# Sparse attention in whole steps: another order of scores, copies, masks and exponentials on three engines

## The chip, the cores and the metric

The kernel runs on one core of a Trainium2 chip. The metric is the device time of one execution in microseconds, the median of several runs.

## The reference

A two-layer decoder trunk over 1024 positions of width 1024, in float32. Layer 0 has latent attention with a convolution beside it, layer 1 native sparse attention; each is followed by a mixture of 32 experts. The change lies in the sparse attention of layer 1. It has 16 heads of width 64 in two groups that share keys and values. The two branches of it that matter here are, cut to their core:

```python
# selected blocks: 8 of 16 blocks of 64 keys for every query
s = einsum('bghqd,bgqnld->bghqnl', qc, kg) * DK ** -0.5 - slopes * dist
p = softmax(where(valid, s, NEG_INF))
o_slc = einsum('bghqnl,bgqnld->bghqd', p, vg)
# sliding window: the last 256 keys
s = einsum('bghqd,bgkd->bghqk', qc, kb) * DK ** -0.5 - slopes * dist
o_win = einsum('bghqk,bgkd->bghqd', softmax(where(valid, s, NEG_INF)), vb)
o = g[0] * o_cmp + g[1] * o_slc + g[2] * o_win
```

## The kernel before, in words

`attend` is called twice: by `mla_attention` for layer 0 (one branch a step, named mlaatt in the trace) and by `nsa_attention` for layer 1 (two branches, nsaatt). A step is one pair of heads (h = 0, 1) and one tile of 128 queries. The sparse attention has 8 pairs, and in each the tiles in the order 0, 7, 1, 6, 2, 5, 3, 4, so 64 steps in 8 rounds. Branch 0, the selected blocks, is computed over all t + 1 causal blocks of 128 keys with a mask that leaves out what wasn't chosen; branch 1, the window, over at most three blocks. A step is *wide* when branch 0 has more than 512 columns (tiles 4 to 7), else *narrow*; wide and narrow steps alternate, and step s + 4 is of the same kind as step s.

The work of a step, by engine:

- TensorE, `score(s, r)`: two or more matmuls into PSUM for branch r and both heads (line 1031). Each head has two banks; a wide branch 0 fills both, a narrow one the first, and the window always uses the second. So a score waits on `masked`, a count of masks that VectorE has done.
- VectorE, `mask(s, i)`, i = 2r + h: adds the mask, takes the maximum, and writes the result from PSUM to `probs` (line 1125). `biased(s, r)` makes the bias of the exponential from the maximum (line 1134).
- ScalarE, `exps(s, r, h)`: the exponential with its sum (line 1083), after `bias_ready`.
- VectorE, `inverse(s, r)`: reciprocal of the sum (line 1139), after `exp_done`. GpSimd scales `probs` with it and the gate (line 1112).
- TensorE, `turn(n)`: transposes a group of up to two blocks and both heads into one of three PSUM banks (line 1041). It needs the scaled rows and the copy of group n - 3.
- ScalarE or VectorE, `copy_group`: copies a transposed group to SBUF (line 1087 on ScalarE, 1005 on VectorE). `by_act[n] = n % 4 != 2`, so VectorE has every fourth group. A round has 34 groups: steps of tiles 0, 7, 1, 6, 2, 5, 3, 4 have 2, 6, 2, 6, 4, 5, 4, 5 of them. Which group of a tile is VectorE's therefore repeats every second round.
- TensorE, `value(n)`: the group's values (line 1054), after its copy; the first of a step waits for the `add` of the step before, since one bank holds the values.
- VectorE, `add(s)`: adds the values to the output (line 1145).

Every engine works its queue strictly in the order of the program. The steps overlap: while TensorE has the values of step s, it makes the scores of step s + AHEAD (4 in the sparse attention, 3 in layer 0), and ScalarE has the exponentials of s + 3. An opening loop fills the first four steps. The loop over s then issues for each step:

| engine | order before, narrow step | order before, wide step |
|---|---|---|
| TensorE | score(s+4, 0), score(s+4, 1), values(s), turns(s+1) | score(s+4, 0), values(s), score(s+4, 1), turns(s+1) |
| ScalarE | four exps(s+3), then its copies(s+1) | the same |
| VectorE | masks 0, 1, 2, biased 0, mask 3, add, both inverses, biased 1, copies | masks 0, 1, add, biased 0, masks 2, 3, both inverses, biased 1, copies |

After a stage's block all engines meet; then `project_out` follows, and the experts' weights of layer 1 are issued behind it on SyncE.

Of the kernel before, what the change touches and what calls it, by code (L numbers as in the profile page):

```python
# [952 lines left out]
def attend(nc, name, steps, ident, loads=None, prepare=None, room=None):  # L953

    S = len(steps)
    BR = len(steps[0]["branches"])
    SUB = 2 * BR
    LAST = BR - 1
    AHEAD = 3 if BR == 1 else 4
# [7 lines left out]
    first = np.cumsum([0] + [len(g) for g in groups]).tolist()  # L967
# [5 lines left out]
    def wide(s):  # L973
        return BR > 1 and steps[s]["branches"][0]["blocks"] * P > BANK

    with Phase(nc, name) as ph:
        probs = ph.sb("probs", [P, BUFS, 2, WIDE])
        outside = room.shape[1] // BANK if room is not None else 0
# [28 lines left out]
        with nc.Block() as block:  # L1007
# [6 lines left out]
            def _(pe):  # L1014
# [47 lines left out]
                for n in range(first[1]):  # L1062
                    turn(n)
                for s in range(S):
                    if s + AHEAD < S:
                        score(s + AHEAD, 0)
                        if BR > 1 and not wide(s + AHEAD):
                            score(s + AHEAD, 1)
                    for n in range(first[s], first[s + 1]):
                        value(n)  # L1070
                    if s + AHEAD < S and wide(s + AHEAD):
                        score(s + AHEAD, 1)
                    if s + 1 < S:
                        for n in range(first[s + 1], first[s + 2]):
                            turn(n)

            @block.scalar
            def _(act):
                def exps(s, r, h):
                    if h == 0:  # L1080
                        act.wait_ge(bias_ready, BR * s + r + 1)
                    b, i = s % BUFS, 2 * r + h
                    act.activation(part(s, r, h), part(s, r, h), ACT.Exp, bias=bias[:, b, i:i + 1], scale=steps[s]["scale"][h],  # L1083
                                   accum_out=total[:, b, i:i + 1]).then_inc(exp_done, 1)

                def copy(to, source):
                    return act.activation(to, source, ACT.Copy)  # L1087

                for s in range(AHEAD - 1):
                    for i in range(SUB):  # L1090
                        exps(s, i // 2, i % 2)
                for n in range(first[1]):
                    if by_act[n]:
                        copy_group(act, copy, n, copied_act)
                for s in range(S):
                    if s + AHEAD - 1 < S:
                        for i in range(SUB):
                            exps(s + AHEAD - 1, i // 2, i % 2)
                    if s + 1 < S:
                        for n in range(first[s + 1], first[s + 2]):  # L1100
                            if by_act[n]:
                                copy_group(act, copy, n, copied_act)

            @block.gpsimd
            def _(pool):
# [10 lines left out]
            def _(dve):  # L1116
# [29 lines left out]
                    else:  # L1146
                        dve.tensor_copy(to, o_ps[:, 0:P]).then_inc(added, 1)

                def copies(s):
                    for n in range(first[s], first[s + 1]):  # L1150
                        if not by_act[n]:
                            copy_group(dve, dve.tensor_copy, n, copied_dve)

                for s in range(AHEAD):
                    for i in range(SUB):
# [3 lines left out]
                    if s:  # L1159
                        for r in range(BR):  # L1160
                            inverse(s - 1, r)
                copies(0)
                for s in range(S):
                    ahead = s + AHEAD < S
                    if ahead:
                        mask(s + AHEAD, 0)
                        mask(s + AHEAD, 1)
                        if BR > 1 and not wide(s + AHEAD):
                            mask(s + AHEAD, 2)
                            biased(s + AHEAD, 0)  # L1170
                            mask(s + AHEAD, 3)
                    add(s)
                    if ahead and wide(s + AHEAD):
                        biased(s + AHEAD, 0)
                        mask(s + AHEAD, 2)
                        mask(s + AHEAD, 3)
                    if s + AHEAD - 1 < S:
                        for r in range(BR):
                            inverse(s + AHEAD - 1, r)
                    if ahead:  # L1180
                        biased(s + AHEAD, LAST)
                    if s + 1 < S:
                        copies(s + 1)


def mla_attention(nc, q_cols, k_cols, v_rows, causal, o_cols, ident, rows_to_clear, loads):
# [1880 lines left out]
```

## Time and profile before

| what | value |
|---|---|
| median of 3 runs | 2205.34 us (2203.54 to 2207.75) |
| the profiled execution, its time | 2202.24 us |
| its span in the trace | 2200.4 us |
| TensorE busy | 1979.2 us |
| sparse attention, both branches | 1320.9 to 1712.2 us |

The times are those of whole executions; the profile is of one of them. A wait in a row of a timeline stands in square brackets: how long the engine was idle before the instruction, and what, by the trace, ended it. Where an engine waits for several semaphores the row names the one that came last by the trace's reckoning, and that can be another than the one that held it. Matmul counts in the trace are passes: a score or value matmul in float32 is two of them, a transpose one.

### The profile page before, as it was taken

Reading aid. Unit: us, or ns where it says so; the run is one execution under the profiler, and the core shown is the slowest. Engines: PE = TensorE matmul, PEld = TensorE weight load, DVE = VectorE, ACT = ScalarE, POOL = GpSimd, SP = SyncE. Lnnn points to the kernel's source line nnn. Section 1 sums busy time; section 2 is a strip of 40 time slices with the busy share of each in tenths; the row PEclk is TensorE's granted clock in tenths of the full one; section 3 lists DMA queues with packets and bytes.
Section 4 is the critical chain, followed back from the end, with each engine's and each line's share of the span. In section 5 each row is a group of like instructions: output and inputs, shape, how many; then the busy total and the mean of one; then the engine's idle time right before and its main releaser. Section 6 shows DMA issues by size and latency. Waiting matters only on the chain. (4 is left out here: it accounts for less than half of the span.)

```text
span 2200.4 us, 30381 instructions
## 1 busy us (share of the span) xinstructions
PE 1979.2 (90%) x11293; PEld 1263.0 (57%) x11293; DVE 951.5 (43%) x2308; ACT 701.0 (32%) x1765; POOL 457.3 (21%) x619
## 2 busy tenths in 40 slices
PE   6999859999999998959999768999999999999887
PEld 3444435655587665645655535666666557766664
DVE  3896974433261211114223486666665125321111
ACT  4013554531111111112122475767666111111110
POOL 0001002331022222100000264445445001222111
PEclk8999969999989999979999988999999999999998
DMA  5000001132588999862000200001000515999992
GB/s 220 0 0 0 0 16 52 36 94 109 211 315 305 375 376 364 307 215 43 1 0 1 80 1 11 11 11 49 11 11 20 195 68 197 340 360 379 377 356 75
DMA packets 80889, 307.78 MB, mean 140 GB/s; under 512 B 18352, under 2 KB 23495, under 8 KB 63846
## 3 DMA queue, kind: packets, MB, share of 16 engines
q1 hardware_dynamic: 66342, 272.23, 32.2%
q0 software_dynamic: 14400, 33.59, 6.2%
q8 instruction: 93, 1.52, 0.3%
q14 instruction: 54, 0.44, 0.1%
HBM read 276.75 MB, written 47.89 MB: 148 GB/s over the span
## 5 line engine op out<-in xcount | busy, mean ns | idle before, releaser
L1112 POOL TENSOR_SCALAR nsaatt_probs<-nsaatt_probs,nsaatt_inv,trunk_gates_or_logits 128x384 f32<-128x384 f32 (+7 forms) x256 | 185.6, 739 | 202.1 <-DVE nsaatt_inv L1139 202.1
L1125 DVE CUSTOM_DVE_ANT_0 nsaatt_probs<-nsaatt_scores,trunk_arena 128x384 f32<-128x384 f32 (+7 forms) x256 | 151.3, 629 | 87.8 <-PE nsaatt_scores L1031 87.5
L1761 DVE TENSOR_TENSOR experts_sig<-experts_gu_ps,experts_sig 128x256 f32<-128x256 f32 x50 | 21.2, 425 | 356.2 <-ACT experts_sig L1718 356.2
L1083 ACT ACTIVATE nsaatt_probs<-nsaatt_probs,nsaatt_bias 128x384 f32<-128x384 f32 (+7 forms) x256 | 169.0, 667 | 11.8 <-DVE nsaatt_bias L1134 11.7
L1594 PEld LDWEIGHTS experts_gu_ps<-experts_x_cols,ahead 128*128 128x128 f32 x1408 | 159.1, 192 | 8.9 <-issue 8.9
L1594 PE MATMUL experts_gu_ps<-experts_x_cols,ahead 128*128 128x128 f32 x1408 | 161.6, 276 | 2.8 <-ACT experts_x_cols L1713 2.8
L1031 PE MATMUL nsaatt_scores<-layer_k_cols,trunk_x_rows 64*128 64x384 f32 (+3 forms) x640 | 131.1, 521 | 15.7 <-DVE nsaatt_top L1125 12.8
L1041 PE MATMUL nsaatt_turn<-trunk_ident,nsaatt_probs 128*128 128x128 f32 x912 | 123.8, 279 | 23.5 <-POOL nsaatt_probs L1112 6.0
L1718 ACT ACTIVATE experts_sig<-experts_gu_ps 128x256 f32<-128x256 f32 x50 | 19.2, 383 | 369.3 <-PE experts_gu_ps L1594 242.5
L1041 PEld LDWEIGHTS nsaatt_turn<-trunk_ident,nsaatt_probs 128*128 128x128 f32 x912 | 97.3, 140 | 57.4 <-issue 37.7
L2239 PE MATMUL nsain_q_ps<-trunk_arena,l1b_h_cols 128*128 128x512 f32 x256 | 111.7, 594 | 0.0
L268 DVE SCALAR_TENSOR_TENSOR l0a_conv<-layer_v_rows,l0a_taps,l0a_conv 128x1024 f32<-128x1024 f32 x87 | 104.8, 1282 | 0.0
L1477 POOL DMA_INDIRECT moe_x<-h_rows,moe_index x46 | 47.5, 1033 | 244.2 <-PE experts_x_ps L1575 229.7
L563 DVE TENSOR_TENSOR trunk_x_rows<-out_acc,trunk_x_rows 128x512 f32<-128x512 f32 x32 | 22.1, 692 | 171.8 <-PE out_acc L491 171.8
L1087 ACT ACTIVATE trunk_arena<-nsaatt_turn 128x512 f32<-128x512 f32 (+1 forms) x136 | 65.8, 514 | 79.7 <-PE nsaatt_turn L1041 79.1
L1031 PEld LDWEIGHTS nsaatt_scores<-layer_k_cols,trunk_x_rows 64*128 64x128 f32 x640 | 55.1, 195 | 60.4 <-issue 37.1
L1722 ACT ACTIVATE trunk_x_rows<-experts_y_ps,moe_gates 128x512 f32<-128x512 f32 x50 | 34.4, 687 | 149.7 <-PE experts_y_ps L1636 75.0
L1054 PE MATMUL nsaatt_values<-trunk_arena,layer_v_rows 128*64 128x128 f32 x1228 | 81.8, 276 | 0.0
L2239 PEld LDWEIGHTS nsain_q_ps<-trunk_arena,l1b_h_cols 128*128 128x128 f32 x256 | 48.2, 190 | 58.0 <-issue 57.9
L1636 PE MATMUL experts_y_ps<-ahead,experts_hid 128*128 128x512 f32 x176 | 79.3, 593 | 2.0 <-DVE trunk_x_rows L1789 2.0
L1031 PE MATMUL mlaatt_scores<-layer_k_cols,trunk_x_rows 96*128 96x512 f32 (+3 forms) x192 | 74.9, 530 | 5.1 <-DVE mlaatt_top L1125 4.1
L1789 DVE TENSOR_SCALAR trunk_x_rows<-experts_y_ps,moe_gates 128x512 f32<-128x512 f32 x50 | 37.4, 748 | 94.6 <-PE experts_y_ps L1636 32.6
(444 smaller groups left out, 3804.2 us busy)
## 6 DMA issues: line engine op xcount, KB each, us to landing
ahead<-in_moe_w_gate_dram SPq DMA_DIRECT2D x34, 1024.0 KB, 14.3
ahead<-in_moe_w_up_dram SPq DMA_DIRECT2D x34, 1024.0 KB, 20.8
ahead<-in_moe_w_down_dram SPq DMA_DIRECT2D x34, 1024.0 KB, 22.1
trunk_arena<-in_moe_w_gate_dram SPq DMA_DIRECT2D x10, 1024.0 KB, 14.0
trunk_arena<-in_moe_w_up_dram SPq DMA_DIRECT2D x10, 1024.0 KB, 18.5
trunk_arena<-in_moe_w_down_dram SPq DMA_DIRECT2D x10, 1024.0 KB, 25.9
moe_w<-in_moe_w_gate_dram SPq DMA_DIRECT2D x10, 1024.0 KB, 12.5
moe_w<-in_moe_w_up_dram SPq DMA_DIRECT2D x10, 1024.0 KB, 23.4
```

The costliest lines, as they stand in the source:

```text
L268: ins = dve.scalar_tensor_tensor(out=to, in0=shifted, scalar=w, in1=to, op0=ALU.mult, op1=ALU.add)
L1031: last = pe.matmul(scores_of(s, r, h)[:, lo:hi], st["q"][h], br["k"][h](lo, hi), start=True, stop=True)
L1041: last = pe.transpose(t_ps[n % TURNS][:, (h * (hi - lo) + b - lo) * P:(h * (hi - lo) + b - lo + 1) * P], part(s, r, h)[:, b * P:(b + 1) * ...
L1054: last = pe.matmul(o_ps[h * V_DIM:(h + 1) * V_DIM, 0:P], br["v"][h](b), turned_probs[n % PT_BUFS][:, at:at + P], start=(r == 0 and b == 0) ...
L1083: act.activation(part(s, r, h), part(s, r, h), ACT.Exp, bias=bias[:, b, i:i + 1], scale=steps[s]["scale"][h], accum_out=total[:, b, i:i + ...
L1087: return act.activation(to, source, ACT.Copy)
L1112: pool.tensor_scalar(part(s, r, h), part(s, r, h), inv[:, s % BUFS, i:i + 1], 1.0 if gate is None else gate[h], ALU.mult, ALU.mult).then_i ...
L1125: dve.tensor_tensor_reduce(part(s, r, h), scores_of(s, r, h), br["mask"], 1.0, -3e38, ALU.add, ALU.max, top[:, s % BUFS, i:i + 1]).then_in ...
L1477: pool.indirect_dma_start(out=x_rows[:, s, :], out_offset=None, in_=h_dram, in_offset=bass.IndirectOffsetOnAxis(ap=rows.bitcast(U32), axis=0),
L1594: last = pe.matmul(to, wm[:, c, half * P:(half + 1) * P], x_cols[:, b, c, :], start=(c == 0), stop=(c == CHUNKS - 1))
L1636: last = pe.matmul(y_ps[half][:, :], hid[:, b, c * P:(c + 1) * P], wm[:, c, half * BANK:(half + 1) * BANK], start=(c == 0), stop=(c == 1))
L2239: last = pe.matmul(to, h_cols[:, c, t * P:(t + 1) * P], w_in[:, c, lo:hi], start=(c == 0), stop=(c == CHUNKS - 1))
```

## The change

Orders alone change, in the loop over s; instructions, buffers and the opening loop are the same. In a step of the sparse attention:

| engine | order after, narrow step | order after, wide step |
|---|---|---|
| TensorE | score(s+4, 0), values(s), score(s+4, 1), turns(s+1) | score(s+4, 0), values(s), turns(s+1), score(s+4, 1) |
| ScalarE | exps 0, 1, two copies, exps 2, one copy, exps 3, the rest | exps 0, 1, 2, copies (five at most), exps 3, the rest |
| VectorE | masks 0 to 3, first copy, biased 0, inverse 0, add, other copies, inverse 1, biased 1 | masks 0, 1, biased 0, add, inverse 0, first copy, mask 2, other copies, mask 3, inverse 1, biased 1 |

With one branch (layer 0) the code has a case of its own, `BR == 1`, with two masks or exponentials in a step.

```diff
+    def copied_by(s, act):
+        return [n for n in range(first[s], first[s + 1]) if by_act[n] == act] if s < S else []
...
                 for s in range(S):
-                    if s + AHEAD < S:
+                    ahead = s + AHEAD < S
+                    if ahead:
                         score(s + AHEAD, 0)
-                        if BR > 1 and not wide(s + AHEAD):
-                            score(s + AHEAD, 1)
                     for n in range(first[s], first[s + 1]):
                         value(n)
-                    if s + AHEAD < S and wide(s + AHEAD):
+                    if ahead and BR > 1 and not wide(s + AHEAD):
                         score(s + AHEAD, 1)
                     if s + 1 < S:
                         for n in range(first[s + 1], first[s + 2]):
                             turn(n)
+                    if ahead and wide(s + AHEAD):
+                        score(s + AHEAD, 1)
...
                 for s in range(S):
-                    if s + AHEAD - 1 < S:
-                        for i in range(SUB):
-                            exps(s + AHEAD - 1, i // 2, i % 2)
-                    if s + 1 < S:
-                        for n in range(first[s + 1], first[s + 2]):
-                            if by_act[n]:
-                                copy_group(act, copy, n, copied_act)
+                    mine = copied_by(s + 1, True)
+                    if BR == 1:
+                        exp_ahead(s, 0)
+                        exp_ahead(s, 1)
+                        copies(mine)
+                    elif wide(s):
+                        exp_ahead(s, 0)
+                        exp_ahead(s, 1)
+                        exp_ahead(s, 2)
+                        copies(mine[:5])
+                        exp_ahead(s, 3)
+                        copies(mine[5:])
+                    else:
+                        exp_ahead(s, 0)
+                        exp_ahead(s, 1)
+                        copies(mine[:2])
+                        exp_ahead(s, 2)
+                        copies(mine[2:3])
+                        exp_ahead(s, 3)
+                        copies(mine[3:])
...
                 for s in range(S):
-                    ahead = s + AHEAD < S
-                    if ahead:
-                        mask(s + AHEAD, 0)
-                        mask(s + AHEAD, 1)
-                        if BR > 1 and not wide(s + AHEAD):
-                            mask(s + AHEAD, 2)
-                            biased(s + AHEAD, 0)
-                            mask(s + AHEAD, 3)
-                    add(s)
-                    if ahead and wide(s + AHEAD):
-                        biased(s + AHEAD, 0)
-                        mask(s + AHEAD, 2)
-                        mask(s + AHEAD, 3)
-                    if s + AHEAD - 1 < S:
-                        for r in range(BR):
-                            inverse(s + AHEAD - 1, r)
-                    if ahead:
-                        biased(s + AHEAD, LAST)
-                    if s + 1 < S:
-                        copies(s + 1)
+                    mine = copied_by(s + 1, False)
+                    mask_ahead(s, 0)
+                    mask_ahead(s, 1)
+                    if BR == 1:
+                        add(s)
+                        inverse_ahead(s, 0)
+                        biased_ahead(s, 0)
+                        copies(mine)
+                    elif wide(s):
+                        biased_ahead(s, 0)
+                        add(s)
+                        inverse_ahead(s, 0)
+                        copies(mine[:1])
+                        mask_ahead(s, 2)
+                        copies(mine[1:])
+                        mask_ahead(s, 3)
+                        inverse_ahead(s, 1)
+                        biased_ahead(s, 1)
+                    else:
+                        mask_ahead(s, 2)
+                        mask_ahead(s, 3)
+                        copies(mine[:1])
+                        biased_ahead(s, 0)
+                        inverse_ahead(s, 0)
+                        add(s)
+                        copies(mine[1:])
+                        inverse_ahead(s, 1)
+                        biased_ahead(s, 1)
```

`exp_ahead`, `mask_ahead`, `biased_ahead` and `inverse_ahead` call the old functions for step s + 3 or s + 4, where there is one; `copies` now takes a list of groups.

## Rows read from the trace of the kernel before

**Rows 1.** The page's first part: busy time of each engine.
```profile
PE 1979.2 (90%) x11293; PEld 1263.0 (57%) x11293; DVE 951.5 (43%) x2308; ACT 701.0 (32%) x1765; POOL 457.3 (21%) x619
```
**Rows 2.** Windows of the sparse attention: whole stage, then its steady part.
```profile
core 0: us, PE busy (x) PEld busy (x) DVE busy (x) ACT busy (x) POOL busy (x), PEclk, DMA share, GB/s
1320.90:1712.20 391.30, 354.55 (x3376) 250.75 (x3376) 241.40 (x912) 262.12 (x716) 185.61 (x256) 0.97 0.06 18
1345.00:1700.00 355.00, 326.85 (x3186) 234.11 (x3184) 225.09 (x848) 246.01 (x673) 175.19 (x241) 1.00 0.06 19
```
**Rows 3.** Waits of TensorE, 1344 to 1712 us: total, times, longest.
```profile
PE nsaatt_scores L1031 <- DVE nsaatt_top L1125: 6.0, 14, 0.5
PE nsaatt_turn L1041 <- POOL nsaatt_probs L1112: 6.0, 8, 1.3
PE nsaatt_turn L1041 <- DVE trunk_arena L1005: 5.7, 6, 1.6
PE nsaatt_turn L1041 <- ACT trunk_arena L1087: 4.5, 8, 0.7
PE nsaatt_turn L1041 <- DVE nsaatt_probs_cols L1005: 3.5, 4, 1.8
PE nsaatt_turn L1041 <- ACT nsaatt_probs_cols L1087: 2.4, 4, 0.7
```
**Rows 4.** Waits of TensorE, 1320 to 1344 us (the opening loop).
```profile
PE nsaatt_scores L1031 <- DVE nsaatt_top L1125: 6.8, 5, 2.6
```
**Rows 5.** Timeline of TensorE: start, length, line, operation, count, wait before it.
```profile
1497.89 2.96 PE L1041 MATMUL nsaatt_turn<-trunk_ident,nsaatt_probs 128*128 128x128 f32 x20
1500.77 1.35 PE L1031 MATMUL nsaatt_scores<-layer_k_cols,trunk_x_rows 64*128 64x512 f32 x8
...
1504.39 0.92 PE L1031 MATMUL nsaatt_scores<-layer_k_cols,trunk_x_rows 64*128 64x384 f32 x4
1505.23 1.31 PE L1041 MATMUL nsaatt_turn<-trunk_ident,nsaatt_probs 128*128 128x128 f32 x10
1507.35 0.41 PE L1041 MATMUL nsaatt_turn<-trunk_ident,nsaatt_probs 128*128 128x128 f32 x2 [0.80 <-POOL nsaatt_probs L1112]
...
1512.00 0.84 PE L1041 MATMUL nsaatt_turn<-trunk_ident,nsaatt_probs 128*128 128x128 f32 x6 [0.68 <-DVE trunk_arena L1005]
...
1529.42 0.92 PE L1031 MATMUL nsaatt_scores<-layer_k_cols,trunk_x_rows 64*128 64x384 f32 x4 [0.41 <-DVE nsaatt_top L1125]
...
1530.85 1.56 PE L1031 MATMUL nsaatt_scores<-layer_k_cols,trunk_x_rows 64*128 64x384 f32 x8
1532.34 0.66 PE L1054 MATMUL nsaatt_values<-nsaatt_probs_cols,layer_v_rows 128*64 128x128 f32 x8
1532.93 1.53 PE L1041 MATMUL nsaatt_turn<-trunk_ident,nsaatt_probs 128*128 128x128 f32 x12
1536.11 1.28 PE L1041 MATMUL nsaatt_turn<-trunk_ident,nsaatt_probs 128*128 128x128 f32 x10 [1.64 <-DVE trunk_arena L1005]
```
**Rows 6.** Timeline of VectorE and ScalarE around two of those waits.
```profile
1506.51 0.69 DVE L1005 COPY nsaatt_probs_cols<-nsaatt_turn 128x512 f32<-128x512 f32 x1
...
1531.28 1.04 ACT L1083 ACTIVATE nsaatt_probs<-nsaatt_probs,nsaatt_bias 128x896 f32<-128x896 f32 x1
...
1533.33 0.61 ACT L1083 ACTIVATE nsaatt_probs<-nsaatt_probs,nsaatt_bias 128x384 f32<-128x384 f32 x1
...
1533.33 0.55 DVE L1125 CUSTOM_DVE_ANT_0 nsaatt_probs<-nsaatt_scores,trunk_arena 128x384 f32<-128x384 f32 x1
...
1534.53 1.07 ACT L1087 ACTIVATE trunk_arena<-nsaatt_turn 128x512 f32<-128x512 f32 x2
1534.67 0.17 DVE L1139 RECIPROCAL nsaatt_inv<-nsaatt_total 128x2 f32<-128x2 f32 x1 [0.50 <-ACT nsaatt_probs L1083]
...
1535.28 0.68 DVE L1005 COPY trunk_arena<-nsaatt_turn 128x512 f32<-128x512 f32 x1
```
**Rows 7.** Timeline of SyncE: the first expert weight load of layer 1.
```profile
1716.45 0.43 SPq L1301 DMA_DIRECT2D ahead<-in_moe_w_gate_dram  x1
```

More of the change, by code:

```diff
@@ L1094, in _, with exp_ahead, copies @@
                         copy_group(act, copy, n, copied_act)
-                for s in range(S):
-                    if s + AHEAD - 1 < S:
-                        for i in range(SUB):
-                            exps(s + AHEAD - 1, i // 2, i % 2)
-                    if s + 1 < S:
-                        for n in range(first[s + 1], first[s + 2]):
-                            if by_act[n]:
-                                copy_group(act, copy, n, copied_act)
+                def exp_ahead(s, i):
+                    if s + AHEAD - 1 < S:
+                        exps(s + AHEAD - 1, i // 2, i % 2)
+                def copies(groups):
+                    for n in groups:
+                        copy_group(act, copy, n, copied_act)
+                for s in range(S):
+                    mine = copied_by(s + 1, True)
[18 more added lines that the diff above has]
+                        copies(mine[3:])
             @block.gpsimd
@@ L1147, in add, with copies @@
                         dve.tensor_copy(to, o_ps[:, 0:P]).then_inc(added, 1)
[L1149 to L1152, printed above, removed]
+                def copies(groups):
+                    for n in groups:
+                        copy_group(dve, dve.tensor_copy, n, copied_dve)
                 for s in range(AHEAD):
@@ L1161, in _ @@
                             inverse(s - 1, r)
-                copies(0)
-                for s in range(S):
-                    ahead = s + AHEAD < S
-                    if ahead:
-                        mask(s + AHEAD, 0)
-                        mask(s + AHEAD, 1)
-                        if BR > 1 and not wide(s + AHEAD):
-                            mask(s + AHEAD, 2)
-                            biased(s + AHEAD, 0)
-                            mask(s + AHEAD, 3)
-                    add(s)
-                    if ahead and wide(s + AHEAD):
-                        biased(s + AHEAD, 0)
-                        mask(s + AHEAD, 2)
-                        mask(s + AHEAD, 3)
-                    if s + AHEAD - 1 < S:
-                        for r in range(BR):
-                            inverse(s + AHEAD - 1, r)
-                    if ahead:
-                        biased(s + AHEAD, LAST)
-                    if s + 1 < S:
-                        copies(s + 1)
+                copies(copied_by(0, False))
@@ new lines, in mask_ahead, with biased_ahead, inverse_ahead @@
+                def mask_ahead(s, i):
+                    if s + AHEAD < S:
+                        mask(s + AHEAD, i)
+                def biased_ahead(s, r):
+                    if s + AHEAD < S:
+                        biased(s + AHEAD, r)
+                def inverse_ahead(s, r):
+                    if s + AHEAD - 1 < S:
+                        inverse(s + AHEAD - 1, r)
+                for s in range(S):
+                    mine = copied_by(s + 1, False)
[26 more added lines that the diff above has]
+                        biased_ahead(s, 1)
```

## The prediction

> **What bounds the kernel.** I read the page first: TensorE is busy 90% of the span, no other engine over 43% [rows 1]. The diff only acts inside the sparse attention, so the next view is the windows: that stage takes 391.3 us, TensorE is busy 354.55 of them and stands at its full clock (1.00) from 1345 to 1700 us, where it is busy 326.85 of 355 us; VectorE, ScalarE and GpSimd are at 62%, 67% and 47% [rows 2]. So TensorE sets the stage's end, and a change of order that leaves its instructions alone can only return its gaps. The waits say how much there is: from 1344 us on, six kinds of wait add up to 28.1 us (6.0 + 6.0 + 5.7 + 4.5 + 3.5 + 2.4): 14 waits of the scores for masks, 30 of the transposes [rows 3]. The 6.8 us of score waits before that [rows 4] belong to the opening loop, which the diff leaves as it is.
>
> Twelve of the 44 waits make up two rounds over the eight tiles: 0.80, 0.68, 0.46, 0.50, 0.41, 1.64 us in one, 0.52, 0.29, 0.46, 0.68, 0.41, 0.75 in the next (four of them, the largest too, are in [rows 5]), 7.6 us together. Rounds differ because a round has 34 groups and every fourth group is VectorE's. I call a round "even" when VectorE has the first and fifth group of tiles 7 and 6, "odd" when it has their third. The wait of 1.64 us is of an even round.
>
> The waits put down to GpSimd are not GpSimd's. The one at 1507.35 us [rows 5] ends 0.15 us after a VectorE copy (1506.51 + 0.69 = 1507.20) [rows 6], and the fourth group must have the first one's copy, since three PSUM banks hold transposes. All 30 waits of transposes are of this kind: a copy stands behind exponentials, masks or reciprocals on its own engine.
>
> **Part 1, wide steps (32 of 64): window scores after the transposes.** Before, a score waits 0.46 or 0.41 us for the masks of its own step, as at 1529.42 us [rows 5]; those 14 waits (6.0 us) go, since the masks are long done when the next step's transposes end. What is late next: these masks start later, and the next narrow step's window scores need them. They come after that step's selected scores and values, at the least 0.65 + 0.59 = 1.24 us later (tile 0, whose partner is tile 2), elsewhere 1.7 us or more. Two masks of 384 columns take 2 x 0.48 us plus 0.2 us of signalling, 1.2 us. It just fits; I allow 0.05 us a step, 1.6 us in all.
>
> With the window scores out of the way, the narrow step's transposes follow the values at once. For tile 2 in an odd round (the 0.80 us wait): values end at 1504.39 us, group 1 some 0.55 us later; VectorE does its add and one reciprocal meanwhile, copies 0.69 us and is done at 1505.8; the fourth group would be reached at 1505.65. About 0.25 us is left of 0.80.
>
> **Part 2, narrow steps (32): window scores after the values.** No instruction is added, but one more run of score matmuls is: a run of 384 columns alone takes 0.84 us (1504.39 to 1505.23), two joined take 1.49 us (1530.85 to 1532.34), so standing alone costs 1.68 - 1.49 = 0.19 us [rows 5]. In a wide step the window scores now run straight into the next step's selected scores, which joins two runs and returns the same 0.19 us. Sum 0; if joining returns nothing, 32 x 0.19 = 6 us lost; if the split costs nothing and joining pays, 6 us won. I take 0, since both prices come from the same two rows. The Trainium skill (TensorEngine Tiling (Array Packing), Key Properties) says that a change of tiling mode drains TensorE; scores use 64 rows, values 64 columns, transposes the whole array. By that rule a narrow step gets one switch more and a wide step one less, the same 0; read as a warning against the split alone it would make the sum 6 us worse, and the trace's 0.19 us agrees with a drain.
>
> **Part 3, ScalarE's copies between its exponentials.** In the worst wait, a narrow step of tile 0 ahead of tile 7: ScalarE does four exponentials, 1531.28 to 1534.53 us, and then two copies [rows 6]. Now it copies after two, at about 1533.35 us or as soon as a group is turned. That is before the fourth group can need it (1534.35, the end of twelve transposes from 1532.93) [rows 5]. The cost is that the last two exponentials end some 1 to 2 us later; cover: their reciprocal feeds GpSimd, whose results are wanted by transposes a whole step later (a pair of steps takes about 11.8 us), and GpSimd is idle for half of the stage. Without that cover it would cost up to 1 us a pair.
>
> **Part 4, VectorE's order.** In the same step the copy of the first group starts at 1535.28 us, behind four masks, the add, both reciprocals (the second waits 0.50 us for ScalarE) and the biases [rows 6]; TensorE goes on at 1536.11 us, 1.64 us late [rows 5]. Afterwards: selected scores alone to 1531.7, values 0.59 to 1532.3, window scores 0.84 to 1533.1, then the transposes. Masks 3 and 4 follow the window scores: 1533.25 + 2 x 0.48 = 1534.2; copy 0.69 to 1534.9; TensorE goes on at 1535.0 and wanted to at 1534.5. So 0.5 us is left of 1.64. In an odd round the first copy is ScalarE's and nothing is left of 0.75. For tile 6, in an even round the same 0.5 us is left. Its twenty transposes hide a wait that no view lists: they take 1497.89 to 1500.77, 2.88 us, where the pitch of 0.115 us and 0.14 us of run-out (twelve transposes are shown with 1.53 us) make 2.44 [rows 5]; 0.44 x 8 rounds = 3.5 us more to be had. For tiles 5 and 4 the first copy comes 1.2 us or more earlier (two exponentials of 0.61 us on ScalarE [rows 6]), against waits of 0.29 to 0.68: nothing and about 0.1 us are left.
> The moved add costs nothing: values of the next step want it only after its scores, 1.3 us or more behind the transposes.
>
> **The sum.** To be had: 28.1 + 3.5 = 31.6 us. Left in two rounds: 0.25 + 0.5 + 0.1 (odd tile 2, even tile 7, tile 4) and 0.5 + 0.15 (tiles 6 and 4 again), 1.5 us, times 4 = 6.0 us. Narrow window scores 1.6 us. Gain 31.6 - 6.0 - 1.6 = 24.0 us. The first attention, with one branch, gets its old order back line for line: 0. After the stage everything is issued behind it in program order, the expert weights too (1716.45 us) [rows 7], so the gain isn't eaten by loads that start at a fixed time; the two loads inside the stage have a DMA share of 0.06 around them [rows 2]. The profiled execution took 2202.24 us (span 2200.4) against a median of 2205.34, 3.1 us or 0.14% apart, so I subtract from the median: 2205.3 - 24 = 2181.3 us, stage about 367 us.
>
> **The rivals.**
> 1. *Half of it* (0.20). VectorE's copies stay late in both kinds of round, since the masks of the window scores now come just when the first group is turned. Then only the score waits (6.0 us) and those put down to ScalarE (4.5 + 2.4) go: 12.9 us, 2192 us. For: the even rounds' remainder above. Against: in odd rounds ScalarE has the first group.
> 2. *The waits only move* (0.06). Values of a wide step need all copies, the last now stand behind the fourth exponential; if TensorE waits there what it waited before, 2205 us. Against: the last copy ends at about 1.6 us into the next step, whose scores and first values take longer.
> 3. *Slower: the narrow window scores wait for VectorE* (0.10). The wide step's masks 3 and 4 now stand behind its transposes and a copy, and the bank is needed 1.24 us later at the earliest. Each 0.1 us by which they are late on all 32 narrow steps costs 3.2 us; from 0.75 us late it eats the 24 us. One 0.69 us copy and a 0.5 us wait for an exponential in front of them make 1.2 us: 2181 + 1.15 x 32 = 2218 us. Against: VectorE is idle 38% of the stage.
> 4. *The likeliest* (0.64): 2181 us, by itself 2173 to 2189 (all waits gone: 31.6 us, 2174; runs of scores dearer by 6 us: 2187).
>
> Range 2173 to 2197: all of the likeliest and rival 1 with some 5 us above it. Measurement can't tell less than 0.2% (4.4 us) from no change. Faster: 0.64 + 0.20 = 0.84; same 0.06; slower 0.10.
>
> **What would show it.** Score waits of 0.4 us gone from the stage; no wait of a transpose over about 0.6 us; the sum of TensorE's waits from 1344 us on down from 28 to 6 to 8 us; runs of eight score matmuls in which 384 columns lead into the next step's; TensorE's busy time within 2 us of 354.55; stage 367 us. I am wrong if scores wait for masks in narrow steps, if values wait for copies, or if TensorE's busy time grows by the 6 us of the extra runs.

## The result, and the profile after

The changed kernel takes 2180.64 us (median of 4 runs, 2177.89 to 2183.09) against 2204.44 us for the kernel before on the same chips: ratio 0.9886, interval 0.9868 to 0.9904, a gain of 23.8 us. The prediction was 2181.3 us.

The page first. TensorE does the same instructions as before [rows 1] and is now busy 91% of a shorter span; the span is 2176.2 us.

```profile
PE 1975.6 (91%) x11293; PEld 1263.9 (58%) x11293; DVE 958.0 (44%) x2308; ACT 700.3 (32%) x1765; POOL 460.0 (21%) x619
```

The windows of the sparse attention, whole and steady, with the columns of [rows 2]. The whole stage takes 366.3 us where it took 391.3; in the steady part TensorE is busy 327.82 of 335 us, 7.2 us short of all, where it was 28 us short of 355. TensorE's busy time over the stage is 350.18 us and not 354.55: 1.9 us of the difference lie outside the steady part that is defined below, most of them in the opening and its clock (last section), 2.5 us inside it.

```profile
1319.80:1686.10 366.30, 350.18 (x3376) 250.71 (x3376) 248.18 (x912) 260.78 (x716) 188.12 (x256) 0.99 0.06 19
1345.00:1680.00 335.00, 327.82 (x3238) 237.95 (x3236) 231.85 (x847) 246.18 (x675) 178.22 (x243) 1.00 0.07 20
```

TensorE's waits from 1344 us to the stage's end, total, times and longest, answer to [rows 3]. The 14 short score waits, the 12 waits of transposes put down to ScalarE and the 8 put down to GpSimd are gone, and of 28.1 us 6.2 are left. (One more wait of a transpose, 0.39 us at 1343.01 us, stands just ahead of this window.) All the remaining waits of transposes are, by the trace, for a copy by VectorE.

```profile
PE nsaatt_turn L1044 <- DVE trunk_arena L1008: 2.3, 7, 0.5
PE nsaatt_turn L1044 <- DVE nsaatt_probs_cols L1008: 1.9, 4, 0.9
PE nsaatt_scores L1034 <- DVE nsaatt_top L1150: 1.2, 1, 1.2
PE nsaatt_values L1057 <- DVE layer_o_all L1170: 0.8, 1, 0.8
```

The timeline of TensorE at the places of [rows 5]. At 1494.07 us the wait of tile 2 is 0.22 us (0.80 before). At 1515.51: eight score matmuls, which are the window scores of a wide step joined with the next step's selected scores (1.49 us for both); values; the window scores alone (0.84 us); then the transposes of tile 7 with 0.46 us of wait in place of 1.64. (A row's length is some 0.07 us more than the step to the row behind it: 1.56 and 1.49 us.) The 20 transposes of tile 6 take 1486.18 to 1488.92, 2.74 us against 2.88.

```profile
1486.18 2.81 PE L1044 MATMUL nsaatt_turn<-trunk_ident,nsaatt_probs 128*128 128x128 f32 x20
...
1494.07 0.41 PE L1044 MATMUL nsaatt_turn<-trunk_ident,nsaatt_probs 128*128 128x128 f32 x2 [0.22 <-DVE nsaatt_probs_cols L1008]
...
1515.51 1.56 PE L1034 MATMUL nsaatt_scores<-layer_k_cols,trunk_x_rows 64*128 64x384 f32 x8
1517.00 0.66 PE L1057 MATMUL nsaatt_values<-nsaatt_probs_cols,layer_v_rows 128*64 128x128 f32 x8
1517.59 0.92 PE L1034 MATMUL nsaatt_scores<-layer_k_cols,trunk_x_rows 64*128 64x384 f32 x4
1518.43 1.53 PE L1044 MATMUL nsaatt_turn<-trunk_ident,nsaatt_probs 128*128 128x128 f32 x12
1520.42 1.28 PE L1044 MATMUL nsaatt_turn<-trunk_ident,nsaatt_probs 128*128 128x128 f32 x10 [0.46 <-DVE trunk_arena L1008]
```

VectorE beside the wait that ends at 1520.42 us. The copy follows the fourth mask at once, and the reciprocal now stands behind it.

```profile
1519.11 0.55 DVE L1150 CUSTOM_DVE_ANT_0 nsaatt_probs<-nsaatt_scores,trunk_arena 128x384 f32<-128x384 f32 x1
...
1519.59 0.69 DVE L1008 COPY trunk_arena<-nsaatt_turn 128x512 f32<-128x512 f32 x1
...
1520.26 0.16 DVE L1164 RECIPROCAL nsaatt_inv<-nsaatt_total 128x2 f32<-128x2 f32 x1
```

For the experiments I use one more measure: the steady part, from the start of the first to the start of the last of the 64 adds of VectorE, in the view of the instructions on the values' PSUM bank. It leaves out the opening, whose clock differs from run to run (the first scores took 1.2 us in some profiles, 0.7 in others). Here it is 1685.6 - 1342.9 = 342.7 us; before it was 1345.4 to 1711.9, 366.5 us. The difference is 23.8 us, the whole gain. The windows view over these two stretches splits it: TensorE's busy time falls by 2.5 us (336.90 to 334.41), its idle time by 21.3 us (29.6 to 8.3).

```profile
L1170 DVE TENSOR_TENSOR layer_o_all<-nsaatt_values,layer_o_all x64: 268/277/292, 1342.9 to 1685.6; 128x128 f32<-128x128 f32 x64
```

The two windows, before and after, with the columns of [rows 2]:

```profile
1345.40:1711.90 366.50, 336.90 (x3314) 242.71 (x3312) 227.60 (x856) 250.89 (x682) 177.62 (x244) 1.00 0.06 19
1342.90:1685.60 342.70, 334.41 (x3304) 243.23 (x3304) 233.75 (x854) 250.03 (x685) 180.11 (x244) 1.00 0.06 20
```

### The profile page after: what moved, and what is told of

The parts are those of the page before. It is cut to its first block and busy times, and to the rows that moved or that the text cites. A ratio compares the mean times of both kernels' runs of the same rounds, so it can differ in the third digit from the quotient of the medians.

```text
span 2176.2 us, 30381 instructions
## 1 busy us (share of the span) xinstructions
PE 1975.6 (91%) x11293; PEld 1263.9 (58%) x11293; DVE 958.0 (44%) x2308; ACT 700.3 (32%) x1765; POOL 460.0 (21%) x619
## 5 line engine op out<-in xcount | busy, mean ns | idle before, releaser
L1044 PEld LDWEIGHTS nsaatt_turn<-trunk_ident,nsaatt_probs 128*128 128x128 f32 x912 | 97.1, 140 | 35.2 <-issue 17.9
L1057 PEld LDWEIGHTS nsaatt_values<-trunk_arena,layer_v_rows 128*64 128x64 f32 x1228 | 67.5, 137 | 20.2 <-issue 12.7
```

What stands on the lines that cost most here:

```text
L1044: last = pe.transpose(t_ps[n % TURNS][:, (h * (hi - lo) + b - lo) * P:(h * (hi - lo) + b - lo + 1) * P], part(s, r, h)[:, b * P:(b + 1) * ...
L1057: last = pe.matmul(o_ps[h * V_DIM:(h + 1) * V_DIM, 0:P], br["v"][h](b), turned_probs[n % PT_BUFS][:, at:at + P], start=(r == 0 and b == 0) ...
```

## The experiments

Nine kernels ran, each timed against the kernel before on its chip. The diffs are against the changed kernel unless they say otherwise. By the code, ScalarE's order alone and TensorE's order alone can't be tried: with VectorE's old order each closes a ring of waits (VectorE waits with its copy for the last exponential or for window scores, and those come behind a fourth group that needs the copy).

| kernel | orders | time, us | ratio to before, interval | steady part, us | TensorE's waits |
|---|---|---|---|---|---|
| before | all old | 2203.7 to 2205.3 | 1 | 366.5 | 28.1 |
| changed | all new | 2180.6 | 0.9886 (0.9868 to 0.9904) | 342.7 | 6.2 |
| x2 | TensorE old | 2205.4 | 0.9997 (0.9987 to 1.0007) | 366.2 | 22.2 |
| x3 | ScalarE old | 2180.9 | 0.9893 (0.9878 to 0.9908) | 341.1 | 5.4 |
| x4 | only VectorE new | 2200.7 | 0.9981 (0.9973 to 0.9990) | 363.3 | 17.9 |
| x5 | narrow scores joined | 2198.6 | 0.9971 (0.9960 to 0.9982) | 359.7 | 20.4 |
| x6 | wide window scores before transposes | 2194.4 | 0.9952 (0.9938 to 0.9966) | 356.4 | 13.5 |
| x7 | VectorE copies third groups | 2179.4 | 0.9878 (0.9863 to 0.9894) | 338.5 | 1.5 |
| x8 | x3 and x7 together | 2173.6 | 0.9860 (0.9839 to 0.9880) | 336.5 | 0.3 |
| x9 | as x3, VectorE's narrow order old | 2186.8 | 0.9916 (0.9901 to 0.9931) | 347.0 | 10.1 |
| x10 | the changed kernel again | 2182.1 | 0.9896 (0.9880 to 0.9912) | 342.8 | 6.6 |

(The waits are the sums of the stage's rows from 1344 to 1712 us as in [rows 3]; a wait of the output projection is left out. The first add of the steady part lies between 1342.8 and 1348.5 us in the executions, so that a wait near 1344 us is counted in some and not in others.)

**x2: TensorE's order taken back.**

```diff
-                    ahead = s + AHEAD < S
-                    if ahead:
+                    if s + AHEAD < S:
                         score(s + AHEAD, 0)
+                        if BR > 1 and not wide(s + AHEAD):
+                            score(s + AHEAD, 1)
                     for n in range(first[s], first[s + 1]):
                         value(n)
-                    if ahead and BR > 1 and not wide(s + AHEAD):
+                    if s + AHEAD < S and wide(s + AHEAD):
                         score(s + AHEAD, 1)
                     if s + 1 < S:
                         for n in range(first[s + 1], first[s + 2]):
                             turn(n)
-                    if ahead and wide(s + AHEAD):
-                        score(s + AHEAD, 1)
```

> TensorE keeps its order of before, ScalarE and VectorE have their new ones. Theory: the gain is copies that come earlier plus score waits that go, and the two add. TensorE's 14 score waits of 0.4 us return (6.0 us), its transposes wait 4 to 5 us as in the changed kernel: 2187 us, 6 us over the changed kernel, ratio to before 0.992. Rival: the place of the window scores is what makes VectorE early, so without it the copies are late again: 2198 us or more.

All of the gain is gone. TensorE's waits in x2:

```profile
PE nsaatt_scores L1034 <- DVE nsaatt_top L1149: 18.7, 34, 1.8
PE nsaatt_turn L1044 <- DVE trunk_arena L1008: 1.9, 7, 0.3
PE nsaatt_turn L1044 <- DVE nsaatt_probs_cols L1008: 1.6, 4, 0.8
```

The waits for copies stay as small as in the changed kernel (3.5 us), but there are 34 waits of scores, up to 1.8 us, where the kernel before had 14 of at most 0.5. VectorE's new wide order puts the window masks behind a copy, so they end later (rows under x4); with the old order of TensorE the next narrow step asks for their bank right after its selected scores. The rival's end came true, for another reason than it gave: the copies weren't late, the masks were. The orders don't add.

The sum of the waits misleads here: it is 5.9 us less than before (22.2 against 28.1), and the time is the same. TensorE's busy time makes up for most of it, 341.31 us in the steady part against 336.90. Nineteen of the waits now stand inside a joined run of scores and split it (see x5).

```profile
1348.00:1714.20 366.20, 341.31 (x3306) 241.27 (x3304) 229.44 (x854) 250.07 (x686) 179.18 (x244) 1.00 0.06 19
```

**x3: ScalarE's order taken back.**

```diff
                 for s in range(S):
-                    mine = copied_by(s + 1, True)
-                    if BR == 1:
...
+                    if s + AHEAD - 1 < S:
+                        for i in range(SUB):
+                            exps(s + AHEAD - 1, i // 2, i % 2)
+                    if s + 1 < S:
+                        for n in range(first[s + 1], first[s + 2]):
+                            if by_act[n]:
+                                copy_group(act, copy, n, copied_act)
```

> ScalarE does all four exponentials before its copies again; TensorE and VectorE have their new orders. Theory: the waits of transposes of 0.3 to 0.75 us come back where ScalarE has the first group, 8 to 12 us in the stage: 2191 us, ratio 0.994. Rival: the copies between exponentials hide nothing, since VectorE's was the late one: 2181 us, as the changed kernel.

The rival was right: the time is that of the changed kernel. TensorE's waits of transposes in x3:

```profile
PE nsaatt_turn L1044 <- DVE trunk_arena L1008: 2.7, 8, 0.5
PE nsaatt_turn L1044 <- DVE nsaatt_probs_cols L1008: 1.9, 4, 0.9
```

No wait is put down to ScalarE, although its copies stand behind four exponentials. Why can be read in the two timelines of ScalarE at the same place, tile 0 ahead of tile 7 in a round where the first group is ScalarE's. Before, ScalarE and then TensorE:

```profile
1578.68 1.03 ACT L1083 ACTIVATE nsaatt_probs<-nsaatt_probs,nsaatt_bias 128x896 f32<-128x896 f32 x1
...
1581.33 0.60 ACT L1083 ACTIVATE nsaatt_probs<-nsaatt_probs,nsaatt_bias 128x384 f32<-128x384 f32 x1
...
1581.93 1.05 ACT L1087 ACTIVATE nsaatt_probs_cols<-nsaatt_turn 128x512 f32<-128x512 f32 x2
```

```profile
1578.29 1.56 PE L1031 MATMUL nsaatt_scores<-layer_k_cols,trunk_x_rows 64*128 64x384 f32 x8
...
1580.37 1.53 PE L1041 MATMUL nsaatt_turn<-trunk_ident,nsaatt_probs 128*128 128x128 f32 x12
```

and in x3, with TensorE's rows below:

```profile
1561.47 1.03 ACT L1087 ACTIVATE nsaatt_probs<-nsaatt_probs,nsaatt_bias 128x896 f32<-128x896 f32 x1
...
1564.12 0.61 ACT L1087 ACTIVATE nsaatt_probs<-nsaatt_probs,nsaatt_bias 128x384 f32<-128x384 f32 x1
...
1564.72 1.07 ACT L1091 ACTIVATE nsaatt_probs_cols<-nsaatt_turn 128x512 f32<-128x512 f32 x2
```

```profile
1561.08 1.56 PE L1034 MATMUL nsaatt_scores<-layer_k_cols,trunk_x_rows 64*128 64x384 f32 x8
...
1564.01 2.81 PE L1044 MATMUL nsaatt_turn<-trunk_ident,nsaatt_probs 128*128 128x128 f32 x22
```

Before, the transposes began at 1580.37 and the first copy at 1581.93 us, 1.56 us later, and TensorE waited 0.75 us. In x3 they begin at 1564.01 and the first copy at 1564.72, 0.71 us later. That is about when the group is ready: at 1486.18 us in the changed kernel, where ScalarE stood idle for it, the first copy began 0.69 us after the transposes. The 22 transposes are one run of 2.81 us without a wait. TensorE's own order makes this room in x3: the window scores between values and transposes put the start of the transposes 0.85 us later against the exponentials (2.54 us after the first one's start in place of 1.69), which start as before, 0.39 us after the joined scores' start in both (1578.68 against 1578.29, 1561.47 against 1561.08). It isn't the only thing that can make it: x4, which follows, has TensorE's old order and ScalarE's old order, and no wait is put down to ScalarE there either.

**x4: only VectorE's order new** (x2 and x3 together).

> Only VectorE has its new order. Theory: score waits (6 us) and ScalarE's late copies (10 us) both stay, VectorE's late copies (about 9 us) go: 2196 us, ratio 0.996. Rival: VectorE's order alone gives all (2181 us), or nothing without the others (2204 us).

2200.7 us and a steady part 3.2 us shorter than before. Waits for VectorE's copies fall to 1.2 us (0.7, and 0.5 for the other copy buffer), score waits rise to 15.6:

```profile
PE nsaatt_scores L1034 <- DVE nsaatt_top L1128: 15.6, 33, 0.8
```

One of the score waits, ahead of tile 7's transposes, on TensorE and on VectorE:

```profile
1388.28 0.92 PE L1034 MATMUL nsaatt_scores<-layer_k_cols,trunk_x_rows 64*128 64x384 f32 x4 [0.40 <-DVE nsaatt_top L1128]
```

```profile
1386.85 0.43 DVE L1008 COPY nsaatt_probs_cols<-nsaatt_turn 128x256 f32<-128x256 f32 x1 [0.64 <-PE nsaatt_turn L1044]
...
1387.67 0.55 DVE L1128 CUSTOM_DVE_ANT_0 nsaatt_probs<-nsaatt_scores,trunk_arena 128x384 f32<-128x384 f32 x1
```

VectorE waits 0.64 us for the transposes of the group that it copies first, and both window masks stand behind that copy; the second ends at 1388.22 us, 0.06 us before TensorE goes on. The window scores that wait for it stand ahead of the values and the transposes, so these start later against ScalarE's exponentials, as in x3, and ScalarE's copies aren't late. By these rows, what ends ScalarE's waits is the distance between exponentials and transposes; in x4 it is paid for with a score wait, in x3 it isn't.

Set beside x2 (2205.4 us, 366.2 against 363.3 us), ScalarE's new order costs 3 us of the steady part when TensorE has its old one (4.7 us by the medians, on one chip), and x2's longest score wait is 1.8 us where x4's is 0.8.

**x5: narrow scores joined ahead of the values** (the price of the split).

```diff
                         score(s + AHEAD, 0)
+                        if BR > 1 and not wide(s + AHEAD):
+                            score(s + AHEAD, 1)
                     for n in range(first[s], first[s + 1]):
                         value(n)
-                    if ahead and BR > 1 and not wide(s + AHEAD):
-                        score(s + AHEAD, 1)
```

> The changed kernel, but in narrow steps both scores stand ahead of the values again, so that the window scores of a wide step, and both scores of the next, follow one another. Theory: the narrow window scores then need the masks of the wide step's window, 1.3 us after its scores, and come after 0.2 to 0.85 us: 28 waits of 0.4 to 1.1 us, 21 us, less 28 runs of scores saved at 0.19 us (5 us): 2180.6 + 16 = 2197 us, TensorE's busy time 5 us lower. Rival: the split of the narrow scores is only a cost: 2175 us.

The theory's 2197 us against 2198.6 measured. The 30 waits of the scores:

```profile
PE nsaatt_scores L1034 <- DVE nsaatt_top L1150: 18.4, 30, 1.2
```

One of them: eight score matmuls (the wide step's window scores and tile 0's selected ones) end at 1460.3 us, then TensorE stands 0.93 us for the masks of the window scores.

```profile
1459.20 1.14 PE L1034 MATMUL nsaatt_scores<-layer_k_cols,trunk_x_rows 64*128 64x384 f32 x8
1461.27 0.49 PE L1034 MATMUL nsaatt_scores<-layer_k_cols,trunk_x_rows 64*128 64x128 f32 x4 [0.93 <-DVE nsaatt_top L1150]
1461.69 1.53 PE L1057 MATMUL nsaatt_values<-trunk_arena,layer_v_rows 128*64 128x128 f32 x24
```

The steady part is 17.0 us longer, the waits 14.2 us: the other 2.8 us are lost although 29 pairs of runs are joined. A wait inside a joined run takes the saving of the join away: from 1459.20 to 1461.69 us are 2.49 us, 1.56 us without the wait, where the changed kernel does the same twelve passes in two separate runs in 1.06 and 0.43 us (from 1494.41 and from 1496.93 us), 1.49 together. The 0.07 us more, at 29 such places, are 2.0 of the 2.8 us, by estimate. The fall of 5 us in busy time that the theory had isn't seen: the score matmuls are busy 115.4 us in the windows view from 1344 to 1720 us, 115.1 in the changed kernel.

**x6: wide window scores ahead of the transposes.**

```diff
-                    if ahead and BR > 1 and not wide(s + AHEAD):
+                    if ahead and BR > 1:
                         score(s + AHEAD, 1)
...
-                    if ahead and wide(s + AHEAD):
-                        score(s + AHEAD, 1)
```

> The changed kernel, but in wide steps the window scores stand between values and transposes as before. Theory: 14 score waits of 0.4 us return (6.0 us) and 28 runs of scores are no longer joined (28 x 0.19 = 5.3 us of busy time): 2192 us, ratio 0.995. Rival: the join returns nothing, only the waits count: 2187 us.

2194.4 us. Waits rise by 7.3 us (6.2 to 13.5), the steady part by 13.8. The scores' waits:

```profile
PE nsaatt_scores L1034 <- DVE nsaatt_top L1148: 8.9, 14, 1.8
```

The 6.5 us that no wait accounts for are 29 runs that are no longer joined (30 wide steps look ahead, and the last has no narrow score behind it), 0.22 us each, near the 0.19 us that [rows 5] give. The windows view goes the same way: score matmuls are busy 123.0 us here against 115.1, 7.9 us more, in which the 0.07 us tail of every row is counted. Joining pays what the split costs.

**x7: VectorE never copies a first group.**

```diff
-    by_act = [n % 4 != 2 for n in range(len(flat))]
+    by_act = [n % 4 != 2 for n in range(len(flat))] if BR == 1 else [k % 4 != 2 for g in groups for k in range(len(g))]
```

> The changed kernel, with the fourth-group rule counted within a step of the sparse attention: VectorE copies the third group of each step that has three or more, 6 groups a round and never the first. Theory: what is left of TensorE's waits for transposes (4.2 us, all behind a VectorE copy of a first group) goes: 2177 us, 0.998 of the changed kernel, ratio to before 0.986. Rival: ScalarE, which has 2.5 copies more a round, becomes the late one: 2181 us or more.

All waits of transposes, 4.2 us, are gone, also those of 0.22 us at the place where one of 0.80 us was put down to GpSimd before; the steady part is 4.2 us shorter. By time alone nothing is shown: the 1.2 us between 2179.4 and 2180.6 are inside the intervals. Of waits, this one and 0.3 us of values for an add are left:

```profile
PE nsaatt_scores L1034 <- DVE nsaatt_top L1150: 1.2, 1, 1.2
```

**x8 to x10: the two findings together, VectorE's narrow order, and the changed kernel again.** x8 has the edits of x3 and x7, x10 none; x9 has that of x3 and this one:

```diff
                         mask_ahead(s, 2)
+                        biased_ahead(s, 0)
                         mask_ahead(s, 3)
-                        copies(mine[:1])
-                        biased_ahead(s, 0)
+                        add(s)
                         inverse_ahead(s, 0)
-                        add(s)
-                        copies(mine[1:])
                         inverse_ahead(s, 1)
                         biased_ahead(s, 1)
+                        copies(mine)
```

> Both findings together: TensorE's and VectorE's new orders, ScalarE's order of before, and VectorE copies the third group of a step. If ScalarE has slack in every step: the steady part takes 338 us or less, 4 us less than in the changed kernel, and the time is 2176 us, ratio to before 0.987. Rival: with every first group ScalarE's, its four exponentials ahead of the copies do hold TensorE, with waits of transposes of 0.3 to 0.7 us in rounds where VectorE had the first group: 2184 us.

> TensorE's new order, VectorE's new order in wide steps only (in narrow steps masks, add, both reciprocals and biases before the copies, as before), ScalarE's order of before. Theory: VectorE's narrow order is what makes its first copies early; without it the waits of 1.6 us at tile 7 and 0.5 to 0.7 us at tile 6 of every second round, and some of tile 5, are back, about 8 us: 2188 us, ratio 0.993. Rival: TensorE's order alone shifts the work enough: 2181 us.

> The changed kernel itself, on the same chip as the other two, to compare them at 0.2%: 2180.6 us, ratio 0.989.

x8 is the fastest, 2173.6 us beside 2182.1 for the changed kernel on the same chip; the steady part is some 6 us shorter (336.5 against 342.8). One wait of 0.3 us is left:

```profile
PE nsaatt_turn L1044 <- ACT trunk_arena L1091: 0.3, 1, 0.3
```

In x9, VectorE's narrow order of before brings waits of up to 1.3 us back, 10.1 us in all with the 0.7 us that is put down to GpSimd, where x3, the same kernel with the new narrow order, has 4.6 of this kind; the steady part is 5.9 us longer. So VectorE's narrow order is worth about 6 us.

```profile
PE nsaatt_turn L1044 <- DVE trunk_arena L1008: 5.8, 10, 0.9
PE nsaatt_turn L1044 <- DVE nsaatt_probs_cols L1008: 3.6, 5, 1.3
```

x10 repeats the changed kernel's waits and its steady part to 0.1 us. Its 6.6 us against 6.2 are the 0.4 us wait that stood ahead of 1344 us in the changed kernel's profile.

## Why the prediction was right, and where only its sum was

**What bounds the stage**: right. TensorE's instructions are the same, its gaps shrank from 28.1 to 6.2 us, and the steady part fell by 23.8 us, by what the median fell. Whether the rest of the kernel gave a little back can't be told: behind the last add the profiled executions take 488.5 us before, 490.6 and 489.9 us in the two of the changed kernel, and 490.8 to 493.0 in the others. The first attention is unchanged: its scores' waits are 5.1 us as before.

**Part 1, window scores behind the transposes**: right. The score waits of 0.4 us are gone. The allowance of 1.6 us for narrow scores that wait for masks was not needed: no such wait is shown. What came in its place is one wait of 1.18 us (ending at 1383.52), in a wide step, and one wait of values for an add in the last steps, 0.8 us; x3 has the second too, and why it comes I can't say. VectorE's rows tell why the first comes: a reciprocal waits 1.29 us for ScalarE's fourth exponential, the preparation of a selection mask (1.21 us, once for each tile) comes behind it, and the masks behind that.

```profile
1379.21 0.17 DVE L1164 RECIPROCAL nsaatt_inv<-nsaatt_total 128x2 f32<-128x2 f32 x1 [1.29 <-ACT nsaatt_probs L1087]
...
1380.14 1.21 DVE L2651 TENSOR_TENSOR trunk_arena<-trunk_arena 128x1024 f32<-128x1024 f32 x1
...
1382.29 1.08 DVE L1150 CUSTOM_DVE_ANT_0 nsaatt_probs<-nsaatt_scores,trunk_arena 128x896 f32<-128x896 f32 x1
```

In x3, with ScalarE's exponentials first, the same reciprocal waits for nothing, the same preparation starts at once, and no score waits. The wait is there in the profiles of x7 and x10, which have ScalarE's new order, and not in x8 and x9, which have the old one.

```profile
1380.62 0.16 DVE L1143 RECIPROCAL nsaatt_inv<-nsaatt_total 128x2 f32<-128x2 f32 x1
...
1380.75 1.22 DVE L2630 TENSOR_TENSOR trunk_arena<-trunk_arena 128x1024 f32<-128x1024 f32 x1
```

**Part 2, the split costs nothing in sum**: right. 0.84 us alone and 1.49 us joined are seen again, x6 prices the missing join at 0.22 us, and the score matmuls are busy 115.1 us after the change and 115.5 before. The drain at a change of tiling mode that the Trainium skill names (TensorEngine Tiling (Array Packing), Key Properties) agrees with it: one switch of mode more in a narrow step, one less in a wide one, and no loss. No run tells a drain from other costs of starting a run. What I had not priced is that the split is needed: joined, narrow scores meet the late masks (x5, 17 us).

**Part 3, ScalarE's copies between its exponentials**: this step failed. I gave it the end of the waits of 0.29 to 0.75 us; x3 has the old order, the same waits and the same time. Those waits ended because the transposes came later against the exponentials: 0.85 us later in x3, by TensorE's order, and in x4 by a score wait. The order is not free either: the reciprocal's wait above is its doing, and I had put its cost at nothing on the strength of GpSimd's slack, where VectorE's queue was the one that felt it. In the steady part it costs 1.6 us (342.7 against 341.1), which the times alone can't tell from zero.

**Part 4, VectorE's order**: right in the place, and nearly in the size. 0.5 us was to be left of 1.64, 0.46 was (0.39, 0.87, 0.46 and 0.46 in the four even rounds); 0.25 of 0.80, 0.22 was; 0.5 for tile 6 in even rounds, 0.38 was; nothing in odd rounds of tile 7. For tile 4, 0.1 to 0.15 us was to be left and no wait is listed. So 4.6 us are left where I had 6.0, the wait at 1343.01 us with them. The 0.87 us in one even round is the 0.46 with a preparation of 0.55 us ahead of VectorE's masks.

**The hidden wait** was there, and the change doesn't end it. I had priced 20 transposes without it at 2.44 us. They take 2.74 us in the changed kernel (from 2.88) and 2.75 even in x8, where no wait of them is listed. So 0.14 us a round was to be had and not 0.44: 1.1 us in all in place of 3.5. What holds them can be read in x8 from TensorE, its weight loads and ScalarE. Tile 6's transposes are the last row of the first fence:

```profile
1515.78 2.81 PE L1044 MATMUL nsaatt_turn<-trunk_ident,nsaatt_probs 128*128 128x128 f32 x22
...
1527.16 2.81 PE L1044 MATMUL nsaatt_turn<-trunk_ident,nsaatt_probs 128*128 128x128 f32 x20
```

```profile
1527.16 1.61 PEld L1044 LDWEIGHTS nsaatt_turn<-trunk_ident,nsaatt_probs 128*128 128x128 f32 x14 [0.55 <-POOL nsaatt_probs L1116]
1529.06 0.68 PEld L1044 LDWEIGHTS nsaatt_turn<-trunk_ident,nsaatt_probs 128*128 128x128 f32 x6 [0.29 <-issue]
```

```profile
1527.86 1.08 ACT L1091 ACTIVATE trunk_arena<-nsaatt_turn 128x512 f32<-128x512 f32 x2 [0.49 <-PE nsaatt_turn L1044]
```

The 22 transposes of tile 7 take no longer than the 20 of tile 6. The weight loads of tile 6, one for each transpose, stop for 0.29 us after 14, which is after its fourth group. The fifth needs the bank of the second, and ScalarE's copy of the second ends at 1528.94 us, 0.12 us before the loads go on. The fourth group of tile 6 is a half one (two transposes, where tile 7 has four), so the fifth comes up sooner than in tile 7. The changed kernel shows the same split into 14 and 6 at 1486.17 us. It is a wait for a copy like the others, short enough that no row of waits lists it; no run tried to end it.

**The total** came out within 0.2 us (24.0 forecast, 23.8 measured in the steady part), and that closeness is partly luck. Of listed waits 21.5 us went (28.1 before, 6.6 after, with the one at 1343.01 us), where the sum had 20.5 (28.1 - 6.0 - 1.6). What else it had was 3.5 us for the hidden wait, and the rest of the measured gain is 2.3 us. Of these 1.1 us can be the hidden wait. The other part is a term that the sum left out: nothing covers the 0.07 us tail of a row ahead of a wait, and there are 30 waits fewer (14 against 44), 2.1 us by estimate. The two together are 0.9 us too much; where that went, nothing here says. Of the signs that I named, two did not come true as stated: one wait of a transpose is over 0.6 us (0.87), and TensorE's busy time over the stage is 4.4 us below 354.55, not within 2 of it.

**The sum over the parts** was right only for all of them together. I worked as if the parts added, score waits and late copies each for itself. x2 and x4 show that VectorE's order with TensorE's old one is worth 0 us (with ScalarE's new order) or 4 us (without). Rival 3, late masks, was the one that this leads to, and its mechanism is what x2 and x5 show; the split in narrow steps is what keeps the changed kernel clear of it.

What stays open: how the 19.5 us of the steady part that x9 gains over the kernel before are shared between TensorE's order and VectorE's wide order. TensorE's alone closes the ring of waits. VectorE's wide order alone, with everything else old, closes no ring that I can see in the code, and it wasn't tried.

## What to carry to other kernels

When engines with strict queues hand work round a ring, an order is a property of all queues together: price a moved instruction by what stands behind it on its own engine and by when the bank that it frees is asked for, and test each queue's order by taking it back alone. Here ScalarE's new order gained nothing, and VectorE's gained 4 us of the 24 without TensorE's. A sum of listed waits isn't the time either: x2 had 5.9 us less of them than the kernel before and took as long. And the cheapest edit was one line, worth 4.2 us of the steady part: don't give the group that the next transposes wait for to the engine whose queue is fullest at that moment.

## What the runs showed of the hardware

- A separate run of score matmuls (64 rows) between values and transposes costs about 0.2 us (0.19 us in [rows 5], 0.22 us in x6). A wait inside a joined run takes the saving of the join away, on top of the wait (x5: 1.56 us without the wait against 1.49 us for the two runs apart; x2: waits 5.9 us less than before, busy time 4.4 us more, the same time).
- The 6.0 us of waits put down to GpSimd in the trace of before behaved as waits for copies. With the orders of the other three engines changed and GpSimd's not, the 0.80 us at tile 2 is 0.22 us and put down to VectorE's copy, and with that copy moved to ScalarE it is gone (x7, x8).
- A wait can be too short for the rows of waits and still repeat in every round: the 0.29 us stop of the weight loads in tile 6's transposes (x8, and the same in the changed kernel) lies behind a copy by ScalarE that ends 0.12 us earlier.
- The opening of the stage is run at a granted clock that differs between executions: 0.58 in its first 20 us in the profile of before, 0.76 in that of the changed kernel. The level isn't the change's doing as far as these profiles show: the first scores took 1.22 us in x7 and 0.71 us in x10, and both have all the changed orders.
